# A row of h with its remainders behind it: one run of 512 columns, and VectorE adds the meta tokens' part

## The reference, cut to what matters

```python
hdn = concat(meta_tokens, x)                     # 16 + 256 tokens
h = rmsnorm(hdn, norm_gain)
q, k, v, f, z_att, u, gate_b, gate_c, z_conv, m_att, m_conv = split(h @ w_in)
c = cumsum(log_sigmoid(f + b_f))
o_att = softmax(q k^T / sqrt(128) + c_t - c_s, causal) v
y_att = (o_att * silu(z_att)) @ w_att_o
o_conv = gate_b * conv3(gate_c * u)              # causal, 3 taps
y_conv = (o_conv * silu(z_conv)) @ w_conv_o
merged = sigmoid(m_att) * y_att + sigmoid(m_conv) * y_conv
out = rmsnorm(hdn + merged @ w_out, final_gain)  # the 256 real tokens alone
```

## Time and profile before

| | |
|---|---|
| Runs | 1199.37, 1200.43, 1200.45 us; median 1200.43 |
| Profiled execution | 1200.54 us, its span 1198.8 us |
| Granted clock of TensorE over the span | 0.998 of 2.4 GHz |
| Busy share: TensorE, VectorE, ScalarE, GpSimd | 99%, 82%, 58%, 2% |
| Memory traffic | 262 GB/s over the span |

### The profile page before, as it was taken

How to read it: one execution, slowest core, us unless ns; L and a number is a source line. 1 busy time by engine, 2 the same in 40 slices (tenths; PEclk the granted TensorE clock), 3 DMA queues, 4 the chain that set the end, 5 groups by cost and what they waited for, 6 DMA issues and landing times.

```text
span 1198.8 us, 18066 instructions
## 1 busy us (share of the span) xinstructions
PE 1187.8 (99%) x7156; PEld 1060.2 (88%) x7156; DVE 988.2 (82%) x1221; ACT 689.4 (58%) x906; POOL 29.3 (2%) x50
## 2 busy tenths in 40 slices
PE   9999999999999999999999999999999999999997
PEld 8998898898898888988988888999999999888886
DVE  6988989989989989989898745787887778788654
ACT  7666656656666666666565644555544554676443
POOL 1000000000000000000000000100100000000000
PEclk9999999999999999999999999999999999999999
DMA  6788798798898897987985878777767777997683
GB/s 216 237 276 299 254 317 287 253 331 268 263 330 275 269 319 266 299 300 262 308 292 190 262 251 262 253 253 236 225 203 243 257 218 241 342 316 256 202 273 121
DMA packets 186564, 315.54 MB, mean 263 GB/s; under 512 B 10257, under 2 KB 121953, under 8 KB 185057
## 3 DMA queue, kind: packets, MB, share of 16 engines
q1 hardware_dynamic: 175408, 296.52, 74.7%
q10 hardware_dynamic: 11072, 17.88, 4.6%
HBM read 294.68 MB, written 19.68 MB: 262 GB/s over the span
## 4 chain that ended last, share of the span: by engine, by line
PE 91%; DVE 6%; issue 1%; ACT 1%; DMA 1%; ACTq 0%; POOLq 0%; POOL 0%; DVEq 0%
PE ps L1827 24%; PE ps L1829 23%; PE ps L1828 23%; PE ps L1843 6%; PE ps L1842 5%; PE ps L1844 3%; PE ps L1841 3%; DVE w_lo L1293 1%; DVE w_lo L1335 1%; DVE w_lo L1323 1%; DMA chan_rows<-in_norm_gain 1%; PE ps L1852 0%; DVE quads L1311 0%; DVE quads L1305 0%; DVE quads L1309 0%
## 5 line engine op out<-in xcount | busy, mean ns | idle before, releaser
L1175 DVE TENSOR_TENSOR w_lo<-w_raw,w_hi 128x1024 fp32r<-128x1024 f32 x172 | 211.9, 1239 | 104.7 <-ACT w_hi L819 104.5
L1827 PE MATMUL ps<-h,w_hi 128*128 128x258 f32 (+1 forms) x1024 | 293.6, 287 | 0.2
L1828 PE MATMUL ps<-h,w_hi 128*128 128x258 f32 (+1 forms) x1024 | 291.3, 284 | 0.0
L1829 PE MATMUL ps<-h,w_lo 128*128 128x258 f32 (+1 forms) x1024 | 291.0, 284 | 0.0
L819 ACT CAST w_hi<-w_raw 128x1024 fp32r<-128x1024 f32 x174 | 182.4, 1050 | 170.8 <-PE ps L1829 116.2
L1827 PEld LDWEIGHTS ps<-h,w_hi 128*128 128x128 f32 x1024 | 192.8, 188 | 2.9 <-issue 0.5
L1828 PEld LDWEIGHTS ps<-h,w_hi 128*128 128x128 f32 x1024 | 192.9, 188 | 2.5
L1829 PEld LDWEIGHTS ps<-h,w_lo 128*128 128x128 f32 x1024 | 192.8, 188 | 0.0
L1293 DVE TENSOR_TENSOR w_lo<-w_raw,w_hi 128x1024 fp32r<-128x1024 f32 x122 | 148.8, 1220 | 16.1 <-ACT w_hi L875 15.9
L875 ACT CAST w_hi<-w_raw 128x1024 fp32r<-128x1024 f32 x122 | 127.8, 1050 | 37.2 <-PE ps L1829 34.1
L1843 PE MATMUL ps<-h,w_hi 128*128 128x512 f32 x340 | 132.8, 396 | 0.0
(11 more groups left out here) (248 smaller groups left out, 2272.0 us busy)
## 6 DMA issues: line engine op xcount, KB each, us to landing
w_raw<-in_w_in SPq DMA_DIRECT2D x210, 512.0 KB, 5.4
quads<-in_w_in SPq DMA_DIRECT2D x168, 512.0 KB, 4.4
w_raw<-in_w_conv_o SPq DMA_DIRECT2D x32, 512.0 KB, 5.5
w_raw<-in_w_out SPq DMA_DIRECT2D x30, 512.0 KB, 5.1
quads<-in_w_in SPq DMA_DIRECT2D x56, 256.0 KB, 4.5
w_raw<-in_w_att_o SPq DMA_DIRECT2D x19, 512.0 KB, 5.6
t_quads<-in_w_att_o SPq DMA_DIRECT2D x8, 1024.0 KB, 6.4
t_dram<-t_quads SPq DMA_DIRECT2D x8, 1024.0 KB, 7.8
```

The costliest lines, as they stand in the source:

```text
L1175: nc.vector.tensor_tensor(w_lo[:, lo_slot(c), :], raw_unit(c), w_hi[:, hi_slot(c), :].bitcast(F32), ALU.subtract).then_inc(w_split, 1)
L1827: nc.tensor.matmul(dst, a_hi, b_hi, start=start, stop=False, skip_group_check=resumed)
L1828: nc.tensor.matmul(dst, a_hi, b_lo, start=False, stop=False, skip_group_check=resumed)
L1829: return nc.tensor.matmul(dst, a_lo, b_hi, start=False, stop=stop, skip_group_check=resumed)
```

## The change

A tile of `h` becomes one row of 640 columns: 16 rounded meta tokens, 256 rounded real tokens, the 256 real tokens' remainders, the remainders of the last two meta tokens, those of the first fourteen. The 512 columns from the first real token on are one run. Products of real tokens (`real_product`) read that. For u and gate_c (`ahead` = 2) and for K, V and f (`ahead` = 16) `row_product` has the same three matmuls with as many columns; the one of the remainders reads from the real tokens on and writes `ahead` columns further, so that the meta tokens' part lands behind the real tokens' sums in PSUM. VectorE copies it to SBUF (`copy_low`) and adds it to the meta tokens' sums (`add_low`, two pieces). ScalarE's `k_hi` and `v_t` now wait for `meta_joined` in place of `w_used`. `cu` is made in two parts. `os_hi` and what follows it, and `x_res` and what follows it, begin 128 bytes further on. Q of pair 0 is turned behind unit 2.

```diff
@@ -50,7 +50,11 @@
 CONV_TOK = SEQ + TAPS - 1
-ROW, ROW_PAD = 320, 64
+ROW, ROW_PAD = 640, 64
+HALO = TAPS - 1
+HI_META, HI_REAL, LO_REAL = slice(0, META), slice(META, TOK), slice(TOK, TOK + SEQ)
+LO_HALO, LO_META = slice(TOK + SEQ, TOK + SEQ + HALO), slice(TOK + SEQ + HALO, TOK + SEQ + META)
+BOTH = slice(META, TOK + SEQ)
...
@@ -376,7 +382,7 @@
     at["h"] += ROW_PAD
-    h = place("h", "h", [P, KT, 2, ROW], F32R)[:].rearrange("p k s n -> p s k n")
+    h = place("h", "h", [P, KT, ROW], F32R)
     o = place("o", "o", [P, 2, KT, SEQ], F32R)
...
@@ -385,7 +391,7 @@
     at["p"] = p_at
-    u_sb = place("p", "u_sb", [P, 2, CONV_TOK])
+    u_sb = place("p", "u_sb", [P, 2, CONV_TOK + HALO])
     cu = place("p", "cu", [P, 2, CONV_TOK])
...
@@ -433,13 +439,13 @@
-    at["h"], at["o"], at["p"] = h_at, o_at, p_at
+    at["h"], at["o"], at["p"] = h_at + 2 * ROW_PAD, o_at, p_at
     os_hi = place("h", "os_hi", [P, STEPS, 4, P], F32R)
     right_c = place("h", "right_c", [P, 2, HALF])
-    at["h"] = h_at
+    at["h"] = h_at + 2 * ROW_PAD
     x_res = place("h", "x_res", [P, 2, D])
...
@@ -1068,7 +1076,7 @@
                     if j == PER:
-                        act.wait_ge(w_used, RING + first + j)
+                        act.wait_ge(meta_joined, META_JOINS["k"] + 2 * i)
                         bank = att_bank(i, K_OF)
...
@@ -1087,7 +1095,7 @@
                     if j == units:
-                        act.wait_ge(w_used, RING + first + j)
+                        act.wait_ge(meta_joined, META_JOINS["v"] + 2 * i)
                         bank = att_bank(i, V_OF)
...
@@ -1175,6 +1183,26 @@
+            def copy_low(rows, bank, blocks, ahead):
+
+                nc.vector.tensor_copy(low[rows, 0:blocks, 0:ahead],
+                                      ps[rows, bank:bank + blocks, SEQ + ahead:SEQ + 2 * ahead]
+                                      ).then_inc(low_copied, 1)
+
+            def add_low(rows, bank, blocks, ahead):
+
+                pieces = [(slice(ahead - HALO, ahead), slice(0, HALO)), (slice(0, ahead - HALO), slice(HALO, ahead))]
+                for toks, behind in pieces[:1 if ahead == HALO else 2]:
+                    total = ps[rows, bank:bank + blocks, toks]
+                    last = nc.vector.tensor_tensor(total, total, low[rows, 0:blocks, behind], ALU.add)
+                return last
+
+            def join_meta(rows, bank, blocks, n):
+
+                copy_low(rows, bank, blocks, META)
+                dve.wait_ge(low_copied, PAIRS + n)
+                add_low(rows, bank, blocks, META).then_inc(meta_joined, 1)
+
             def join(bank, dst):
...
@@ -1228,8 +1256,10 @@
                 dve.wait_ge(meta_rounded, 1)
-                nc.vector.tensor_tensor(h[:, LO, :, 0:META], meta_t[:], h[:, HI, :, 0:META].bitcast(F32),
-                                        ALU.subtract).then_inc(meta_split, 1)
+                for toks, dst in ((slice(META - HALO, META), LO_HALO), (slice(0, META - HALO), LO_META)):
+                    last = nc.vector.tensor_tensor(h[:, :, dst], meta_t[:, :, toks], h[:, :, toks].bitcast(F32),
+                                                   ALU.subtract)
+                last.then_inc(meta_split, 1)
...
@@ -1428,7 +1458,14 @@
                     dve.wait_ge(free[A], FREE_A["conv"] + 2 * pair + 1)
-                    nc.vector.tensor_tensor(cu[:], ps[:, B:B + 2, 0:CONV_TOK], u_sb[:], ALU.mult
+                    copy_low(slice(0, P), B, 2, HALO)
+                    nc.vector.tensor_tensor(u_sb[:, :, 0:HALO], u_sb[:, :, 0:HALO], u_sb[:, :, CONV_TOK:], ALU.add)
+                    dve.wait_ge(low_copied, pair + 1)
+                    add_low(slice(0, P), B, 2, HALO).then_inc(halo_joined, 1)
+                    real = slice(HALO, CONV_TOK)
+                    nc.vector.tensor_tensor(cu[:, :, real], ps[:, B:B + 2, real], u_sb[:, :, real], ALU.mult)
+                    dve.wait_ge(halo_joined, pair + 1)
+                    nc.vector.tensor_tensor(cu[:, :, 0:HALO], ps[:, B:B + 2, 0:HALO], u_sb[:, :, 0:HALO], ALU.mult
                                             ).then_inc(free[B], 1)
...
@@ -1470,6 +1507,8 @@
             dve.wait_ge(w_used, RING + U_F + N_F)
+            join_meta(slice(0, HEADS), C, 1, META_JOINS["f"])
+            dve.wait_ge(meta_joined, META_JOINS["f"])
             dve.wait_ge(bf_landed, 16)
...
@@ -1595,6 +1634,8 @@
                         bank = att_bank(i, K_OF)
+                        dve.wait_ge(w_used, RING + first + j)
+                        join_meta(slice(0, P), bank, 2, META_JOINS["k"] + 2 * i)
                         dve.wait_ge(kq_rounded, 2 * i + (2 if hosted else 1))
...
@@ -1635,6 +1676,9 @@
                         last.then_inc(att_step, 1)
+                        bank = att_bank(i, V_OF)
+                        dve.wait_ge(w_used, RING + first + j)
+                        join_meta(slice(0, P), bank, 2, META_JOINS["v"] + 2 * i)
                     if i > 0 or j > 1:
...
@@ -1780,13 +1823,12 @@
                         hi, lo = w_hi[:, hi_slot(c), w], w_lo[:, lo_slot(c), w]
-                        if cols == SEQ:
-                            last = wide_product(halves(bank + b), hi, lo, src[:, :, k, part],
-                                                start=(k == 0), stop=(k == KT - 1),
+                        if ahead == 0:
+                            last = real_product(ps[:, bank + b, :], hi, lo, k, start=(k == 0), stop=(k == KT - 1),
                                                 narrow_first=(b == blocks - 1 and k > 0))
                         else:
-                            last = product(ps[:, bank + b, 0:cols], hi, lo, src[:, HI, k, part],
-                                           src[:, LO, k, part], start=(k == 0), stop=(k == KT - 1))
+                            last = row_product(ps[:, bank + b, :], hi, lo, k, ahead, start=(k == 0),
+                                               stop=(k == KT - 1))
                         if kk == k_in - 1 and b == blocks - 1:
...
@@ -1835,15 +1877,30 @@
-            def wide_product(dst, a_hi, a_lo, b, start=True, stop=True, narrow_first=False):
-
-                if narrow_first:
-                    nc.tensor.matmul(dst[:, HI, :], a_lo, b[:, HI, :], start=False, stop=False)
-                    return nc.tensor.matmul(dst, a_hi, b, start=False, stop=stop)
+            def wide_product(dst, a_hi, a_lo, b, start=True, stop=True):
+
                 nc.tensor.matmul(dst, a_hi, b, start=start, stop=False)
-            ALL, REAL, CONV = slice(0, TOK), slice(META, TOK), slice(META - TAPS + 1, TOK)
+            ALL, REAL, CONV = META, 0, HALO
+
+            def row_product(dst, a_hi, a_lo, k, ahead, start, stop):
+
+
+
+                hi, lo = slice(META - ahead, TOK), slice(TOK, TOK + SEQ + ahead)
+                nc.tensor.matmul(dst[:, 0:SEQ + ahead], a_hi, h[:, k, hi], start=start, stop=False)
+                nc.tensor.matmul(dst[:, ahead:SEQ + 2 * ahead], a_hi, h[:, k, lo], start=False, stop=False,
+                                 skip_group_check=True)
+                return nc.tensor.matmul(dst[:, 0:SEQ + ahead], a_lo, h[:, k, hi], start=False, stop=stop)
+
+            def real_product(dst, a_hi, a_lo, k, start, stop, narrow_first):
+
+                if narrow_first:
+                    nc.tensor.matmul(dst[:, 0:SEQ], a_lo, h[:, k, HI_REAL], start=False, stop=False)
+                    return nc.tensor.matmul(dst, a_hi, h[:, k, BOTH], start=False, stop=stop)
+                nc.tensor.matmul(dst, a_hi, h[:, k, BOTH], start=start, stop=False)
+                return nc.tensor.matmul(dst[:, 0:SEQ], a_lo, h[:, k, HI_REAL], start=False, stop=stop)
...
@@ -1987,11 +2044,12 @@
                         return nc.tensor.matmul(ps[0:F_LO + HEADS, C, 0:TOK], f_weights(c)[:, kk, 0:F_LO + HEADS],
-                                                h[:, HI, k, ALL], start=(k == 0), stop=(k == KT - 1))
+                                                h[:, k, 0:TOK], start=(k == 0), stop=(k == KT - 1))
                     def f_low_h(k):
-                        return nc.tensor.matmul(ps[0:HEADS, C, 0:TOK], f_weights(c)[:, kk, 0:HEADS],
-                                                h[:, LO, k, ALL], start=False, stop=False)
+                        return nc.tensor.matmul(ps[0:HEADS, C, META:TOK + META], f_weights(c)[:, kk, 0:HEADS],
+                                                h[:, k, TOK:TOK + TOK], start=False, stop=False,
+                                                skip_group_check=True)
...
@@ -2056,10 +2114,10 @@
                         pe.wait_ge(free[bank], att_free(i, which))
-                    project(None, 0, U_ATT + att_first(i) + j, bank, h, REAL if which == Q_OF else ALL, j % PER * UK)
+                    project(None, 0, U_ATT + att_first(i) + j, bank, REAL if which == Q_OF else ALL, j % PER * UK)
                     if i > 0:
                         finish_pair(i - 1, j)
-                    if j == 1 and hosted:
```

(34 more changed lines are left out.)

## The result

The changed kernel takes 1211.79 us (median of 4 runs, 1210.42 to 1212.98), the kernel before beside it 1200.19 (4 runs, 1199.37 to 1200.45): ratio 1.0097, 95% interval 1.008 to 1.0115. Slower by 11.6 us; forecast were 7.9, and 1208.3 us with a range of 1202 to 1213. The side and most of the mechanisms were right, two terms of the sum were not, and the range held in part by luck.

A forecast was written before the change was run, and what follows sets the result against it. TensorE was taken to set the pace, except in second halves of hosted groups, where VectorE does. Terms: 8.4 (V) + 2.5 (convolution) - 0.8 - 0.8 (one run) - 0.5 (`os`) - 0.9 (Q) = +7.9 us: 1208.3 us, range 1202 to 1213.

The forecast's parts named there:

- (a): Real-token products in Q and the convolution: one 512-column run saves 6 ns each, 0.8 us in Q, 0.8 in pairs 0 and 7.
- (b): Remainders' products with 258 or 272 columns start and write elsewhere: taken as nothing, between -3.7 and +3.7 us.
- first rival: Where rows of `h` start sets the cost; new rows save 5 ns each, -14 us, 1194.3 us in all; chance 0.08.
- (c): `os_hi` and `os_lo` moved by 128 bytes: 96 products 6 ns faster each, -0.5 us, if the address is the cause.
- (d): Convolution, VectorE's split `cu` and small additions: 0.4 us more each, moving L1410 in pairs 1 to 6, 2.5 us.
- (e): Attention, K: `k_hi` waits some 0.6 us for VectorE's copy and adds, still in time; costs nothing.
- (f): Attention, V: `v_t` waits for VectorE's join behind the scaling; TensorE stands still 1.04 us per pair, 8.4 us.
- (g): Start and forget gate: `split_meta` 0.1 us longer, a join of 16 rows 0.6 us; costs nothing.
- (h): Pair 0's turning of Q moves behind unit 2, so TensorE no longer waits for `partial`: -0.9 us.
- third rival: Small instructions don't overlap and K's join delays what follows: +14 us and 1214, half way 1211 likelier; chance 0.14.
- second rival: VectorE finishes scaling before V's last unit ends, so the V stall goes and 1199.9 us is left; chance 0.11.
- fourth: Rival: new layout gives nothing, two runs and one cost the same, `os` too; 1210.4 us; chance 0.05.

The follow-up runs named there:

- e5: Changed kernel, but the 512-column product in `real_product` reads the unit's own rounded weights `w_hi` in place of `h`; 1212.96 us (one run).
- e6: Kernel before with one part of the change alone: `os_hi`, `os_lo` and `x_res` begin 128 bytes further on; 1199.61 us (one run).
- e4: Changed kernel without VectorE's additions in the convolution, `cu` one instruction again; 1210.54 us, ratio to the kernel before 1.0087.
- e1: Changed kernel, but in each attention pair's last round VectorE joins V before it scales the probabilities; 1205.07 us, ratio to the kernel before 1.0045.
- e7: Kernel before with `os` and `x` 128 bytes further on and Q of pair 0 turned behind unit 2; 1198.59 us, ratio 0.9984.
- e3: Changed kernel, but the remainders' product reads from 2 (16) columns earlier and writes where it did; 1209.68 us.
- e8: Kernel before, but the remainders' product reads only the 256 real tokens, leaving out the meta tokens' remainders; 1198.5 us (one run).
- gap of 48: Changed kernel with 48 unused columns between rounded tokens and their remainders in every row of `h`; 1208.98 us (one run).

## Why the prediction was right on the side and short in size

- **(a) One run of 512: failed.** Taken: -1.6 us. Measured: nothing (233.1 ns before, 233.1 and 233.3 after, 233 even with `w_hi` in e5). The step that failed is the comparison of two rows that differed in more than the runs: those at 396 ns alternate with 256-column products, those at 391 follow each other. The formula of the Trainium skill, TensorE: Matmul & The Clock Gate, section Back-to-back issue gap, has the number of columns alone in it and so the same price for both forms, as measured here. Its size is not: the section gives N / 2.4 + 2.5, 216 ns, for an isolated warm matmul and about 131 ns for 512 columns in a stream with weight loads, and the trace has 227 to 233.
- **(b) Remainders' products: failed.** Taken: nothing, between -3.7 and +3.7. Measured: +4.9 us in the rows, outside the bounds. "The length read is the same" was true, but the place read from was not, and the bound was drawn from 256 against 258 columns, a difference of length. The first rival looked in the right place (where the row is read) and had the wrong sign. By which rule the address acts stays open.
- **(c) `os`: right.** -0.5 forecast (its own 96 x 6 ns are 0.58), -0.6 in e6.
- **(d) Convolution: right mechanism, smaller term.** 0.33 us a pair where 0.4 was taken, 2.0 us where 2.5; e4 shows that it moves the group nearly one for one. (The estimate by the Trainium skill, VectorE: DVE Perf Modes, section The TRN2 errata, was 0.65 us for four instructions in a row; the trace has the overlap of the earlier trace rows and half of that.) Where it would show was wrong: the wait at the boundary stayed at 0.5 us, and the lateness appears at the split L1323 instead. The period of 84.3 became 84.67; of the 0.73 over before e4 ascribes 0.32 to the additions, and the rest is the size of (b).
- **(e) K: right.** `k_hi` waits for VectorE eight times, and TensorE never waits for `k_hi`.
- **(f) V: right mechanism, term mis-sized.** 8.4 us forecast, 6.7 measured. Taken were 0.64 us for the join and 0.12 for TensorE's start behind ScalarE; measured 0.51 and 0.05. (The row that the 0.12 came from gives 749.17 - 749.02 = 0.15.) VectorE was also free 0.07 us earlier against TensorE's arrival. e1 gives all of it back by moving three lines.
- **(g), (h): right.** Q of pair 0: -0.9 forecast, -0.8 in the traces, and no idle time in e7.

By terms: 6.7 + 2.0 + 4.9 - 0.6 - 0.8 = 12.2 us from the first product on, 12.0 in the traces (the 0.8 of the hosted chains not counted), 7.9 forecast. The sum was short by the 4.9 of (b) and the 1.6 of (a), and too long by 1.7 of (f) and 0.5 of (d). That 1211.79 lies within 1202 to 1213 is in part luck: the upper end was drawn for the third rival (small instructions that don't overlap), while (d) and (f) came out cheaper than forecast and what filled the room was (b), whose bound was passed. The lower end takes -2.5 us for (b), whose stated bound is -3.7; with that it would be 1201.1.

The second rival, V not late, fell with the first trace. The third's total (1211 to 1214) was met without its mechanism. The fourth (the layout gives nothing, 1210.4) was half true: the run gave nothing, the shift of `os` did.

## What to carry to other kernels

When a result that another engine waits for gains a step on a busy in-order engine, the place of that step in the engine's order costs more than the step: here 0.5 us of additions stood behind 1.9 us of scaling, and moving three lines was worth 7 us. When a layout changes, compare start-to-start distances of every matmul that reads it, the unmoved ones too, and take a price for a form of read only from rows that differ in nothing else.

## What the runs showed of the hardware that was not expected

- A matmul's price depends on what ran ahead of it. In the 258-column rows the third product, with unmoved operands, went from 119.1 to 126.4 ns when the second's read moved from 1280 to 1032 bytes behind the first's; shifting that read by 2 columns (e3) put 124.8 on the second and 116.3 on the third. Nine 512-column products behind a 258-column unit took 2064 ns before, 2079 after and 2047 in e8, and with e8 none of their operands moved.
- Stationary operands moved by 128 bytes: 394 to 396 ns a record became 389, 233 ns from start to start became 227, 96 products, 0.6 us (e6).
- Products of 512 columns came every 227 ns in the earlier trace rows and every 233 ns next to products of 256 columns, whether they read one run, two, or `w_hi` (e5); but also every 233 ns among themselves (`os` before), and every 228.1 next to 256 columns in one of the two groups with a gap of 48. The neighbour alone does not set the price.
- The start of the first product of `h` varies by 1.5 us (14.78 in e1, 16.29 in after) between executions of kernels whose start is the same, so a difference of 1 us between the times of two single runs says little.
